# Wider value products, paired score products and an earlier weight load in a three-part transformer kernel

## What is computed

```python
def mla_layer(x, cos, sin, norm_g, w_in, q_norm_g, w_q_b, kv_norm_g, w_kv_b, w_out):
    h = rmsnorm(x, norm_g)
    proj = h @ w_in
    q_lat, kv_lat, k_rope, z = proj[..., :o1], proj[..., o1:o2], proj[..., o2:o3], proj[..., o3:]
    q = (rmsnorm(q_lat, q_norm_g) @ w_q_b).reshape(B, S, N_HEADS, QK_HEAD_DIM)
    kv = (rmsnorm(kv_lat, kv_norm_g) @ w_kv_b).reshape(B, S, N_HEADS, QK_NOPE_DIM + V_HEAD_DIM)
...
ATT_PATTERNS = ((128, 1), (512, 4), (2048, 16))   # window, dilation; 8 heads of 64

def attention_mixer(z):
    qkv = z.reshape(b, s, ATT_GROUPS, 3, ATT_HEADS, ATT_HEAD_DIM)
    for g, (window, dilation) in enumerate(ATT_PATTERNS):
        o, l = dilated_window_attention(qkv[:, :, g, 0], qkv[:, :, g, 1], qkv[:, :, g, 2], window, dilation)
...
    scores = jnp.einsum('bnqrhe,bnkrhe->bnrhqk', qb, kc) * (e ** -0.5)
    scores = jnp.where(valid[None, :, None, None], scores, -jnp.inf)
    m = jnp.max(scores, axis=-1, keepdims=True)
    p = jnp.exp(scores - m)
    den = jnp.sum(p, axis=-1)
    num = jnp.einsum('bnrhqk,bnkrhe->bnqrhe', p, vc)
```

## Time and profile before

| | us |
|---|---|
| median of 3 runs | 2622.35 (2617.26 to 2622.53) |
| the profiled execution | 2624.49 |
| its span, first to last instruction | 2622.8 |
| PE busy / PEld busy | 2417.0 (92%) / 1957.0 (75%) |
| DVE / ACT / POOL busy | 1321.7 / 597.5 / 1036.1 |
| share of the chain that ended last: PE, DVE, issue | 69%, 13%, 8% |
| mean granted TensorE clock | 0.946 of 2.4 GHz |

### The profile page before, as it was taken

The page is one execution under the profiler, slowest core; times in us unless marked ns, Lnnn a source line. Parts: engine busy times, 40 slices in busy tenths (PEclk is TensorE's granted clock), DMA queues, the critical chain, the costliest instruction groups (busy, mean ns, idle before and its releaser), DMA issues.

```text
span 2622.8 us, 32892 instructions
## 1 busy us (share of the span) xinstructions
PE 2417.0 (92%) x12476; PEld 1957.0 (75%) x12476; DVE 1321.7 (50%) x1720; ACT 597.5 (23%) x1275; POOL 1036.1 (40%) x768
## 2 busy tenths in 40 slices
PE   5999997999988899999979999999998898999598
PEld 4887876776746787979758888988887677777486
DVE  5888333554553412010275565555654546888612
ACT  2100012333331113020222233323332202222101
POOL 3876744343305551414132112211211465666363
PEclk8999998999978898979889999999999999999798
DMA  3223312434332220202021111011102332222121
GB/s 100 89 90 96 109 51 75 148 97 148 107 97 94 80 77 21 80 17 97 11 70 40 35 43 52 25 35 44 35 1 90 100 109 68 93 81 94 45 88 60
DMA packets 183334, 189.49 MB, mean 72 GB/s; under 512 B 8093, under 2 KB 167468, under 8 KB 182956
## 3 DMA queue, kind: packets, MB, share of 16 engines
q1 hardware_dynamic: 175312, 181.81, 22.0%
q10 hardware_dynamic: 7900, 5.94, 0.8%
HBM read 179.30 MB, written 8.44 MB: 72 GB/s over the span
## 4 chain that ended last, share of the span: by engine, by line
PE 69%; DVE 13%; issue 8%; DVEq 4%; POOL 3%; ACT 1%; DMA 1%; POOLq 1%; ACTq 0%; SPq 0%
PE bank L1228 8%; PE bank L741 8%; PE bank L743 8%; PE bank L742 8%; DVEq L2368 3%; PE bank L1054 2%; POOL wlo L602 2%; PE bank L863 2%; PE bank L865 2%; PE bank L864 2%; PE bank L943 2%; PE bank L1037 1%; PE bank L1036 1%; PE bank L1035 1%; PE bank L1123 1%
## 5 line engine op out<-in xcount | busy, mean ns | idle before, releaser
L602 POOL TENSOR_TENSOR wlo<-raw,whi 128x1024 fp32r<-128x1024 f32 (+5 forms) x316 | 684.7, 2167 | 47.3 <-issue 5.8
L600 POOL TENSOR_SCALAR whi<-raw 128x1024 fp32r<-128x1024 f32 (+5 forms) x316 | 326.2, 1032 | 772.7 <-PE bank L1125 308.5
L741 PE MATMUL bank<-hbuf,whi 128*128 128x512 f32 x904 | 359.2, 397 | 29.0 <-ACT cpad L1818 17.0
L743 PE MATMUL bank<-hbuf,wlo 128*128 128x512 f32 x904 | 355.3, 393 | 0.0
L576 POOL TENSOR_TENSOR spare<-ones 1x1 f32<-1x1 f32 x104 | 28.9, 278 | 730.0 <-PE bank L743 466.7
L742 PE MATMUL bank<-hbuf,whi 128*128 128x512 f32 (+2 forms) x776 | 304.9, 393 | 0.0
L741 PEld LDWEIGHTS bank<-hbuf,whi 128*128 128x128 f32 x904 | 170.2, 188 | 78.3 <-issue 28.2
L743 PEld LDWEIGHTS bank<-hbuf,wlo 128*128 128x128 f32 x904 | 170.3, 188 | 38.1
L2101 DVE TENSOR_REDUCE nmax<-bank 128x4 f32<-128x512 f32 (+3 forms) x40 | 21.6, 557 | 323.6 <-PE bank L1056 323.6
L742 PEld LDWEIGHTS bank<-hbuf,whi 128*128 128x128 f32 (+2 forms) x776 | 146.4, 189 | 31.1
L2297 DVE TENSOR_TENSOR hf<-bank,hf 128x512 f32<-128x512 f32 (+1 forms) x96 | 53.5, 558 | 158.3 <-PE bank L1228 156.8
(11 more groups left out here) (470 smaller groups left out, 5697.9 us busy)
## 6 DMA issues: line engine op xcount, KB each, us to landing
adaw<-in_w_ada SPq DMA_DIRECT2D x64, 384.0 KB, 4.0
raw<-in_w_up SPq DMA_DIRECT2D x22, 1024.0 KB, 5.1
raw<-in_w_in SPq DMA_DIRECT2D x41, 512.0 KB, 4.0
raw<-in_w_in SPq DMA_DIRECT2D x18, 1024.0 KB, 5.1
raw<-in_pool_w_in SPq DMA_DIRECT2D x16, 1024.0 KB, 5.6
raw<-in_mla_w_in SPq DMA_DIRECT2D x10, 1024.0 KB, 6.4
raw<-in_pool_w_out SPq DMA_DIRECT2D x8, 1024.0 KB, 5.2
raw<-in_mla_w_out SPq DMA_DIRECT2D x8, 1024.0 KB, 5.1
```

Of the source, the lines that this page charges most:

```text
L600: G.tensor_scalar(h_, r_, 1.0, 1.0, ALU.mult, ALU.mult)
L602: G.tensor_tensor(l_, r_, f32(h_), ALU.subtract).then_inc(raw_split, 1)
L741: M.matmul(dst, wh, acts[k][0], start=(first and k == 0), stop=False)
L743: mm = M.matmul(dst, wl, acts[k][0], start=False, stop=(last and k == n - 1))
```

## The change

There are three. The attention's strips are grouped by group (3 turns of 6 strips), and a value strip now holds 512 input rows of all 512 value columns, so value matmuls move 512 columns and accumulate over two strips in four banks, one for each block of 128 tokens; ScalarE copies all four after the second strip. The units are ordered by pairs of heads; the scores of two heads are made together, in alternate row halves and two banks, followed by one wide mask each, and four banks (4, 5, 0, 1) take scores. SP's wait ahead of the heads' strips is for the norm n_mla, which is long past there, in place of n_kv.

```diff
@@ -59,7 +59,7 @@
-          ("att", 9, 2), ("lora", 1, 2), ("rkv", PAIRS, 3), ("mix", 4, 2), ("wo", 2, 2), ("up", 11, 2),
+          ("att", 3, 6), ("lora", 1, 2), ("rkv", PAIRS, 3), ("mix", 4, 2), ("wo", 2, 2), ("up", 11, 2),
...
@@ -141,13 +141,13 @@
-    units = []
-    for h in range(ATT_HEADS):
-        if g == 0:
-            units += [(h, [(0, 0), (1, 0), (1, 1)]), (h, [(2, 1), (2, 2), (3, 2), (3, 3)])]
-        else:
-            units.append((h, [(b, b) for b in range(4)]))
-    return units
+    parts = [[(0, 0), (1, 0), (1, 1)], [(2, 1), (2, 2), (3, 2), (3, 3)]] if g == 0 else [[(b, b) for b in range(4)]]
+    return [(h, blocks) for t in range(ATT_HEADS // 2) for blocks in parts for h in (2 * t, 2 * t + 1)]
+
+
+def score_slot(U):
+
+    return (4, 5, 0, 1)[U % 4]
...
@@ -429,7 +429,9 @@
             if ph == "att":
-                return w_in2[:, :, ds(i * 512 + j * 256, 256)], 8, 256
+                if j < 4:
+                    return w_in2[:, :, ds(i * 1536 + j * 256, 256)], 8, 256
+                return w_in2[:, (j - 4) * 4:(j - 3) * 4, ds(i * 1536 + 1024, 512)], 4, 512
...
@@ -480,7 +482,7 @@
                 if ph == "heads":
-                    sp.wait_ge(sem("norm.lo"), NORM0["n_kv"]["lo"] + 2)
+                    sp.wait_ge(sem("norm.lo"), NORM0["n_mla"]["lo"] + DT)
...
@@ -1019,42 +1021,54 @@
                 for j in range(2):
-                    strip_ready(sg + 4 + j, 1)
-                    for hv in range(2):
-                        b = j * 2 + hv
-                        bank_free("att", b, 3 * g + 2)
-                        for t in range(2):
-                            blk = hv * 2 + t
-                            dst = bank[b][:, t * 256:(t + 1) * 256]
-                            for k in range(DT):
-                                if g == 0:
-                                    ah, al = [x[:, blk * P:(blk + 1) * P] for x in h_out[k]]
-                                else:
-                                    ah, al = [x[:, blk:S:4] for x in h_out[k]]
-                                wh, wl = whi[j][:, k * 256:(k + 1) * 256], wlo[j][:, k * 256:(k + 1) * 256]
-                                M.matmul(dst, ah, wh, start=(k == 0), stop=False)
-                                M.matmul(dst, ah, wl, start=False, stop=False)
-                                mm = M.matmul(dst, al, wh, start=False, stop=(k == DT - 1))
-                        mm.then_inc(products_done, 1)
+                    for blk in range(4):
+                        if j == 0:
+                            bank_free("att", blk, 3 * g + 2)
+                        for k in range(4):
+                            if blk == 0 and k in (0, 2):
+                                strip_ready(sg + 4 + j, k // 2)
+                            tokens = slice(blk * P, (blk + 1) * P) if g == 0 else slice(blk, S, 4)
+                            ah, al = [x[:, tokens] for x in h_out[j * 4 + k]]
+                            wh, wl = whi[j][:, k * S:(k + 1) * S], wlo[j][:, k * S:(k + 1) * S]
+                            M.matmul(bank[blk][:, :], ah, wh, start=(j == 0 and k == 0), stop=False)
+                            M.matmul(bank[blk][:, :], ah, wl, start=False, stop=False)
+                            mm = M.matmul(bank[blk][:, :], al, wh, start=False, stop=(j == 1 and k == 3))
+                        if blk % 2 == 1:
+                            mm.then_inc(products_done, 1)
...
                 def scores(u):
-                    h, blocks = units[u]
                     U = units_before + u
-                    if U >= 2:
-                        pe.wait_ge(sem("att.exp"), U - 1)
-                    dst, rows = bank[4 + U % 2], slice((h % 2) * 64, (h % 2) * 64 + 64)
-                    for qb, kb0, nk, c0 in att_rows(blocks):
-                        w = nk * P
-                        mask = neg_dil[:, :] if g == 2 else neg_band[:, (2 - nk) * P:2 * P]
-                        base = (h // 2) * S
-                        M.matmul(dst[:, c0:c0 + w], aq[rows, base + qb * P:base + (qb + 1) * P],
-                                 ak[rows, base + kb0 * P:base + kb0 * P + w], start=True, stop=False)
-                        mm = M.matmul(dst[:, c0:c0 + w], ident_b[:, :], mask, start=False, stop=True)
-                    mm.then_inc(sem("att.s"), 1)
+                    if U >= 4:
+                        pe.wait_ge(sem("att.exp"), U - 2)
+                    blocks = units[u][1]
+                    base = (units[u][0] // 2) * S
+                    for n, (qb, kb0, nk, c0) in enumerate(att_rows(blocks)):
+                        for h in range(2):
+                            rows = slice(h * 64, h * 64 + 64)
+                            M.matmul(bank[score_slot(U + h)][:, c0:c0 + nk * P],
+                                     aq[rows, base + qb * P:base + (qb + 1) * P],
+                                     ak[rows, base + kb0 * P:base + (kb0 + nk) * P],
+                                     start=(n == 0), stop=False, skip_group_check=True)
+                    for h in range(2):
+                        dst = bank[score_slot(U + h)]
+                        if g:
+                            mask = neg_dil[:, :] if g == 2 else neg_causal
+                            mm = M.matmul(dst[:, :], ident_b[:, :], mask.unsqueeze(1).to_broadcast([P, 4, P]),
+                                          start=False, stop=True, skip_group_check=True)
+                        elif len(blocks) == 4:
+                            mm = M.matmul(dst[:, :], ident_b[:, :],
+                                          neg_band[:, :].unsqueeze(1).to_broadcast([P, 2, 2 * P]),
+                                          start=False, stop=True, skip_group_check=True)
+                        else:
+                            M.matmul(dst[:, 0:P], ident_b[:, :], neg_band[:, P:2 * P], start=False, stop=True,
+                                     skip_group_check=True)
+                            mm = M.matmul(dst[:, P:3 * P], ident_b[:, :], neg_band[:, :], start=False, stop=True,
+                                          skip_group_check=True)
+                        mm.then_inc(sem("att.s"), 1)
...
                     U = units_before + u
-                    first = h % 2 == 0 and (u == 0 or units[u - 1][0] != h)
+                    first = u == 0 or units[u - 1][0] // 2 != h // 2
                     pe.wait_ge(sem("att.te"), U + 1)
...
                 for u in range(len(units) + 2):
-                    if u < len(units):
+                    if u < len(units) and u % 2 == 0:
                         scores(u)
                     if 1 <= u <= len(units):
                         turned(u - 1)
@@ -1569,14 +1583,12 @@
-                for j in range(2):
-                    for hv in range(2):
-                        b = j * 2 + hv
-                        product_ready(sg + 4 + j, hv)
-                        x = bank[b][:, :].rearrange("p (k r par e) -> p k r par e", k=2, r=2, par=2)
-                        for par in range(2):
-                            cp = A.copy(av6[:, 2 * hv:2 * hv + 2, 2 * j:2 * j + 2, par, par, :], x[:, :, :, par, :])
-                        cp.then_inc(evac[b], 1)
+                for b in range(4):
+                    product_ready(sg + 5, b // 2)
+                    x = bank[b][:, :].rearrange("p (r par e) -> p r par e", r=4, par=2)
+                    for par in range(2):
+                        cp = A.copy(av6[:, b, :, par, par, :], x[:, :, par, :])
+                    cp.then_inc(evac[b], 1)
...
                 def pair_ends(u):
-                    return units[u][0] % 2 == 1 and (u + 1 == len(units) or units[u + 1][0] != units[u][0])
+                    return u + 1 == len(units) or units[u + 1][0] // 2 != units[u][0] // 2
...
-                            ex = A.activation(ap_[U % 2][:, c0:c0 + nk * P], bank[4 + U % 2][:, c0:c0 + nk * P],
+                            ex = A.activation(ap_[U % 2][:, c0:c0 + nk * P], bank[score_slot(U)][:, c0:c0 + nk * P],
                                               ACT.Exp, bias=nmax[:, n:n + 1], accum_out=den[:, n:n + 1])
...
```

## The result

The changed kernel takes 2537.2 us (median of 5 runs, 2533.4 to 2548.3) where the kernel before takes 2622.35: ratio 0.968, 95% interval 0.9654 to 0.9706, or 85 us less. The forecast was 2532, range 2516 to 2556. Two later jobs with the same kernel gave 2540.3 (0.9679, 0.9641 to 0.9718) and 2533.6 (0.9703, 0.9663 to 0.9744). Two executions far above the rest, one of the changed kernel in the second of these jobs (11197.1 us) and one of before in the same job (2783.3 us), are left out of the medians and means of this text.

The account below looks back on a forecast made before the run. TensorE was taken as the bound, busy nearly all the time in the touched stages. Savings of 46.2 (v), 38 (attention) and 5.7 (heads' loads) sum to 89.9 us off 2624.49: 2534.6, forecast as a median of 2532, range 2516 to 2556.

Parts of the forecast that it names:

- The v products: Value matmuls of three groups: 96 of 512 columns replace 192 of 256, saving 1.4, 22.4 and 22.4 us, 46.2 in all.
- the rival of a visible load: Value products: the wide matmul doesn't hide its weights load, 0.34 us each, total 2553 us; chance 0.08.
- The attention's work: Three attention stages without half clock: 45.7, 31.1 and 31.1 us fall to 40, 25 and 25.
- The pair: Two heads in groups 1 and 2: 4.5 us of PE work plus 0.8 of waiting, 5.3 in place of 7.3.
- pairs serial: Paired scores: records come one after another without overlap, 0.8 us for each of 16 pairs, total 2545; chance 0.09.
- ScalarE bound: Attention: ScalarE's exponentials and num copy also stall PE for the second head, 1.5 us for each of eight pairs, 2544; chance 0.08.
- The clock in the attention: Attention stages: 7 us at half clock in each group, +3.0 us each, giving stages of 43, 28, 28, 38 us saved.
- the gap at a stage's start: Start of the attention stages: the new gap after v is longer than before, so the clock falls again.
- The heads' loads: First head: the q load goes earlier, PE starts at 442.8 in place of 449.0; gain 5.7 us, bounds 4.4 and 7.7.
- The 0.5 for a collision of POOL and VectorE: Before the first head: the early q split meets VectorE's last q norm sum, costing 0.5 us, at most 1.80.
- Nothing outside these stages changes: Rest of the kernel: what follows the third group starts from its end and shifts whole.
- The slower rival: Projections behind the attention: the fallen clock doesn't rise there either, +192 us, total 2724; chance 0.01.

Follow-up runs that it names:

- third profile: The changed kernel, unedited, run and profiled a third time: median 2533.6 us, profiled span 2531.0 us.
- the earlier scores: The changed kernel with each pair's scores issued one unit earlier, ahead of the transposes of the unit before: 2531.0 us (0.9639), run again 2534.0 (0.9682).
- the pairs-only kernel: The kernel before with the paired scores and whole-bank masks alone, value products and SP's wait as before: 2578.0 us (0.9818).
- the first profile: The changed kernel's first profiled execution: 2548.25 us, span 2546.5, where the kernel before has a span of 2622.8.

## Why the prediction was right, point by point

**The v products**, 46.2 forecast, 46.2 measured (1.45 and twice 22.35), and 45.5 with the part alone. The reason holds too: with contiguous tokens the 44.9 become 23.4. The 512-column stream hides behind the load or the load behind it; the rival of a visible load (0.34 apart) is out, at 0.235.

**The attention's work.** Without half clock the forecast took the stages from 45.7, 31.1 and 31.1 to 40, 25 and 25, 17.9 less. Measured: no half clock in group 0, 38.5, nor in group 2 of the third profile, 24.6; group 1, which always had 3.4 us of it, is put at 24.9 by the same difference, an estimate. That is 19.9 less. The pair is right to 0.02 us (5.28 for 5.3), with both terms: 1.54 for scores and masks (forecast 1.65), a wait of 0.78 on ScalarE (0.8). Group 0 was put too high: 8.78 for two heads where I had 9.0, since its two waits of 0.5 were 0.62 and 0.17. The rivals "pairs serial" and "ScalarE bound" are out, the second by the earlier scores as well.

**The clock in the attention** is the term that was mis-sized. I took 7 us at half clock in each group, 21 in all, down from 67.6; it was 0, 3.4 and 3.4. Of the 47.8 us that the stages fell by, 19.9 are work, so the clock gave 27.9 and not 20, where 38 was forecast for both. That the gap at a stage's start makes the clock fall is not borne out as a rule. It fell behind the wait of 2.1 in five of six such stages in three profiles, and not in the sixth; it never fell with the scores ahead, where the wait is 0.48. In group 0 two waits of 1.5 passed without a fall, while the pairs-only kernel had one of 3.4 us there, with a first wait of 0.94.

**The heads' loads.** 442.93 for 442.8, and ScalarE as what is late next. The 0.5 for a collision of POOL and VectorE came as 0.44 (the sum of 1.13 us for 0.69), in all three profiles of the changed kernel and with the new wait alone; PE's wait for it went from 1.18 to 1.6. In the first profile it can't be seen further on, since the z products behind it ran fewer of their matmuls at half clock: the next norm's factors stand at 437.62 where they stood at 437.65. Over the three profiles the q product came 6.1, 6.1 and 5.1 us earlier, where 5.7 was forecast. In the first PE then ran 6.1 us at half clock where it was 4.6, so part of that was given back.

**The step that failed** is the sentence "Nothing outside these stages changes". It is true of the work (the same 2121 and 7035 records) and false of the time: the rest took 23.8 us more in the profiled execution and about 13 on average. The forecast of 2532 lies 5 us from the median because two errors of 10 and 13 us have opposite signs. That is luck. With the stages right and this step as it was I would have said 2522, outside every run of the changed kernel.

**The slower rival** (half clock into the projections) is out: their clock is 1.00 in every version.

## What to carry to other kernels

Where 64-row and 128-row matmuls alternate, count the changes of form before the columns: gather what has one form, put the two halves side by side, and add a mask once for a whole bank. Where a weights load reads with a stride, give each load more columns to stream until the stream is as long as the load. A kernel with a tenth of its span at half clock pays for a saving in one stage partly elsewhere: add up the half clock of the whole span, in several executions, before a gain is put down to a stage.

## What was not expected of the hardware

- The sum of half clock outside the changed stages differed by 55 us between profiles (217 to 271), worth 23 us of time, while the changed kernel's medians lie within 7 us of each other and those of before within 3. Among the 60 executions of before, the half clock read from the mean granted clock goes with 84% of the variance of the time, at 0.37 us for a microsecond.
- The two profiles of before have the same stretches in the attention to a tenth of a microsecond in length, while the same attention code behind another v stage, or 6 us earlier, has others (13.6, 37.5 and 17.1 against 0, 27.3 and 30.7). A stage's clock is no property of its code alone: the changed kernel's group 2 had 3.4 us at half clock in two profiles and none in the third.
- Four 64-row score records between two 128-row masks take the 0.42 us that two take.
- The strided weights load took 329 ns under 256-column matmuls and 309 under 512-column ones, against 187 to 192 contiguous.
